# Next layer's norm and first weights made in the last down projection, rotary tables in the load stage, output projections begun by parts

## The reference

```python
    for l in range(DEPTH):
        h = rms_norm(x, norm_mix[l])
        z = h @ w_in[l]
        ...
        mix = jnp.concatenate([o_att, o_hg.astype(x.dtype), o_cv], axis=-1)
        x = x + mix @ w_out[l]

        h = rms_norm(x, norm_mlp[l])
        x = x + jnp.square(jax.nn.relu(h @ w_mlp_in[l])) @ w_mlp_out[l]
    return x
```

## Time and profile before

| | us |
|---|---|
| median of 3 runs | 4067.52 |
| lowest, highest | 4065.33, 4071.44 |
| the profiled execution | 4068.66 |
| its span, first to last instruction | 4066.5 |
| PE busy in it | 3733.8 (92%) |
| DVE, ACT, POOL busy | 2072.0, 1319.8, 1283.6 |

### The profile page before, as it was taken

One profiled execution on the slowest core, in us unless ns is written; L12 is line 12 of the kernel. 1 busy time (PEld: TensorE's weight loads), 2 busy tenths in 40 slices (PEclk: granted clock), 3 DMA queues, 4 the chain that ended last, 5 costly groups with the idle time before them and its releaser, 6 DMA issues. The chain is left out here.

```text
span 4066.5 us, 46227 instructions
## 1 busy us (share of the span) xinstructions
PE 3733.8 (92%) x17918; PEld 2842.7 (70%) x17918; DVE 2072.0 (51%) x2990; ACT 1319.8 (32%) x2225; POOL 1283.6 (32%) x522
## 2 busy tenths in 40 slices
PE   7888999887899979999999989998899999989997
PEld 5555888665578857676777668886657777668885
DVE  4886555398654533533263465443352255345453
ACT  5344111343421121434333421112254433332112
POOL 2202444330144423132323244442113232224442
PEclk9889999997999989999999999999999999899998
DMA  3101333220023232121212123333212122113322
GB/s 111 52 11 42 99 94 93 74 63 16 26 94 94 93 108 86 36 64 57 81 55 73 47 78 94 98 93 112 59 32 78 58 72 68 57 59 95 97 93 67
DMA packets 80145, 292.58 MB, mean 72 GB/s; under 512 B 9616, under 2 KB 10928, under 8 KB 79408
## 3 DMA queue, kind: packets, MB, share of 16 engines
q1 hardware_dynamic: 77136, 278.49, 22.0%
q10 hardware_dynamic: 2784, 11.03, 0.8%
HBM read 285.30 MB, written 2.10 MB: 71 GB/s over the span
## 5 line engine op out<-in xcount | busy, mean ns | idle before, releaser
L207 POOL TENSOR_TENSOR w_lo<-w_raw,w_hi 128x1024 fp32r<-128x1024 f32 x518 | 1283.4, 2478 | 2736.7 <-ACT w_hi L193 2736.6
L193 ACT ACTIVATE w_hi<-w_raw 128x1024 fp32r<-128x1024 f32 x518 | 549.1, 1060 | 1828.7 <-PE acc L244 1757.8
L242 PE MATMUL acc<-hH,w_hi 128*128 128x512 f32 x1840 | 778.5, 423 | 130.9 <-DVE hL L305 70.1
L244 PE MATMUL acc<-hL,w_hi 128*128 128x512 f32 x1840 | 732.0, 398 | 0.0
L243 PE MATMUL acc<-hH,w_lo 128*128 128x512 f32 x1840 | 731.7, 398 | 0.0
L242 PEld LDWEIGHTS acc<-hH,w_hi 128*128 128x128 f32 x1840 | 355.5, 193 | 232.1 <-issue 111.7
L275 DVE TENSOR_TENSOR xT<-acc,xT 128x512 f32<-128x512 f32 x160 | 110.7, 692 | 639.5 <-PE acc L244 639.5
L242 PE MATMUL acc<-H,w_hi 128*128 128x512 f32 x1024 | 405.8, 396 | 5.9 <-issue 4.2
L243 PEld LDWEIGHTS acc<-hH,w_lo 128*128 128x128 f32 x1840 | 355.4, 193 | 76.5 <-issue 12.0
L244 PEld LDWEIGHTS acc<-hL,w_hi 128*128 128x128 f32 x1840 | 353.7, 192 | 78.0
L242 PE MATMUL acc<-midH,w_hi 128*128 128x512 f32 x1024 | 403.7, 394 | 4.2 <-issue 4.2
(11 more groups left out here) (325 smaller groups left out, 4578.5 us busy)
## 6 DMA issues: line engine op xcount, KB each, us to landing
w_raw<-in_stream SPq DMA_DIRECT2D x518, 512.0 KB, 3.5
cw<-in_cmpw ACTq DMA_DIRECT2D x2, 2048.0 KB, 7.9
mixed<-in_cmpw ACTq DMA_DIRECT2D x2, 2048.0 KB, 14.0
x_tok<-in_x SPq DMA_DIRECT2D x1, 2048.0 KB, 9.0
out<-f_tok SPq DMA_DIRECT2D x4, 512.0 KB, 2.6
stack<-Z ACTq DMA_DIRECT2D x8, 128.0 KB, 3.6
stack<-Z ACTq DMA_DIRECT2D x8, 127.8 KB, 3.7
masks_f<-in_masks SPq DMA_DIRECT2D x1, 960.0 KB, 10.8
```

Of the source, the lines that this page charges most:

```text
L193: act.activation(w_hi[:, u % WB, 0:w], w_raw[:, u % 2, 0:w], ACT.Copy).then_inc(hi_split, 1)
L207: pool.tensor_tensor(w_lo[:, u % WB, 0:w], w_raw[:, u % 2, 0:w], w_hi[:, u % WB, 0:w], ALU.subtract)\
L242: pe.matmul(acc[n % 2][:, :], wh, H[:, k, :], start=(k == 0), stop=False)
L244: last = pe.matmul(acc[n % 2][:, :], wh, Lo[:, k, :], start=False, stop=(k == nk - 1))
```

## The change

1. **Norm of the next layer in the last `down`.** `mlp_act` and `mlp_dve` do in the last group `down3` what `out` does: after each `add_to_x` the tile is scaled with the next layer's norm weights (`norm_next`, new columns of `vec`), squared, split into `hH`, `hL`, and the squares are added. A layer begins with one matmul over the added squares (`sum_squares`) and the factor (`rstd_act`), and PE waits for no k part. The buffers `tmp`, `pair`, `yt` are now allocated once.
2. **First weights of the next layer.** `load_next` loads units 0 and 1 of the next layer (new inputs `next1`, `next2`) behind the last units, `split_hi_next` and `split_lo_next` split unit 0. The next layer splits unit 1 first and loads from unit 2 on.
3. **Load stage.** It now also makes the second kind's tables (own buffers `cos2`, `sin2`), the first layer's norm, its unit 0 and the load of unit 1. x comes in two halves, and waits are split by what is needed. `start_second` is gone.
4. **`out` by parts.** Tiles 0 and 1 are each made in two pieces, early k of both, then late k of both (`Group.some`). In a first layer the early k are 4, 5, 0, 1, 2 and the late 3, 6, 7, each with its own wait. In a second layer the early k are 0 to 3; `take_last` splits each tile of `mixed` right after its sum.
5. **`store_result`** has its squares already, releases each `f_y` tile singly, transposes by halves of the width, and stores 8 pieces in place of 4.

```diff
-                        pe.wait_ge(lo_split, u + 1)
+                        if u:
+                            pe.wait_ge(lo_split, u)
...
+            def some(self, tile, ks, ready, begin, end):
+                u, t, n = self.tiles[tile]
...
+                for j, k in enumerate(ks):
+                    ready(k)
...
+        def out_pe(units, early, late, ready):
             out_tiles = Group(units, "out")
+            for ks in (early, late):
+                for tile in range(2):
+                    out_tiles.some(tile, ks, ready, ks is early, ks is late)
+            del out_tiles.tiles[0:2]
             out_tiles.products()
...
+        def load_next(units, source, L):
+            n = len(units)
+            for u in range(2):
+                last_user = n - 2 + (u - n) % 2
+                sp.wait_ge(lo_split, last_user)
+                sp.dma_start(w_raw[:, u, :], source[bass.ds(L, 1), u].rearrange("a p n -> (a p) n"))\
+                    .then_inc(next_loaded[u], 16)
+            for u in range(2):
+                sp.wait_ge(next_loaded[u], 16)
+        def split_hi_next(units):
+            n = max(x[3] for u, x in enumerate(units) if u % WB == 0)
+            act.wait_ge(acc_ready[n % 2], n // 2 + 1)
+            act.wait_ge(next_loaded[0], 16)
+            act.activation(w_hi[:, 0, :], w_raw[:, 0, :], ACT.Copy).then_inc(hi_split, 1)
...
+            def added(k):
+                n = first + k
+                ahead.split_ahead(1)
+                if k == NK - 1:
+                    split_hi_next(units)
+                act.wait_ge(acc_free[n % 2], n // 2 + 1)
+            scale_act(1, gcol, y, sq, added)
...
+        def add_and_scale(r, tiles, y, hi, lo, sq):
+            for k in range(NK):
+                tiles.evacuate(add_to_x, 1)
+                if k:
+                    scale_dve(r, y, hi, lo, k - 1)
+                    add_square(r, sq, k - 1)
+            scale_dve(r, y, hi, lo, NK - 1)
+            add_square(r, sq, NK - 1)
...
                     def _(pe):
                         finish(pe, "start")
                         first_in = Group(units, "first_in")
-                        first_in.products(1, h_ready(0), square_sums(0, pair))
+                        sum_squares(pair)
                         first_in.products()
...
                         finish(pe, "att")
-                        after(pe, stages, "att", act_finished, dve_finished)
-                        out_pe(units, pair)
+                        pe.wait_ge(conv_mean, 2)
+                        pe.wait_ge(conv_rstd, 1)
+                        def out_ready(k):
+                            if k < 4:
+                                pe.wait_ge(att.o_free, k + 1)
+                            if k >= 6:
+                                pe.wait_ge(conv_split, k - 5)
+                        out_pe(units, [4, 5, 0, 1, 2], [3, 6, 7], out_ready)
...
                     def _(act):
-                        split_hi(units, 0)
                         split_hi(units, 1)
+                        act.preload_act_table_set(LOG_EXP)
+                        rstd_act(1)
+                        split_hi(units, 2)
                         act.wait_ge(vec_loaded, 16)
-                        scale_act(0, V1["norm_mix"], yt, pair)
-                        split_hi(units, 2)
...
                         def take_last(i, a, free, value):
                             dve.wait_ge(gate_opened, 3 * NK + i + 1)
                             add_branch(3, i, Z0[:, i, :], a, free, value)
+                            dve.wait_ge(branch_mixed, 3 * NK + i + 1)
+                            link(dve, dve.tensor_copy(hH[:, i, :], mixed[:, i, :]))
+                            dve.tensor_tensor(hL[:, i, :], mixed[:, i, :], hH[:, i, :], ALU.subtract).then_inc(out_split, 1)
                         Group(units, "mix3").evacuate(take_last)
-                        for k in range(NK):
-                            split_dve(hH[:, k, :], hL[:, k, :], mixed[:, k, :])
...
         load_start()
         with nc.Fori(0, DEPTH) as L:
             first_layer(L)
-        start_second()
         with nc.Fori(0, DEPTH) as L:
             second_layer(L)
         store_result()
```

More of the change, by code:

```diff
@@ L349, in h_ready @@
             return lambda k: pe.wait_ge(h_split, NK * r + k + 1)
-        def square_sums(r, sq):
-            def sums(k):
-                pe.wait_ge(sq_ready, NK * r + k + 1)
-                pe.matmul(B[0][:, :], ones, sq[:, k % 2, :], start=(k == 0), stop=(k == NK - 1)).then_inc(sq_summed, 1)
-            return sums
         def split_dve(hi, lo, src):
@@ L390, in mlp_dve @@
                 Group(units, f"up{b}").evacuate(hidden)
-                Group(units, f"down{b}").evacuate(add_to_x)
+                if b < FB - 1:
+                    Group(units, f"down{b}").evacuate(add_to_x)
+            add_and_scale(1, Group(units, f"down{FB - 1}"), y, hH, hL, sq)
         def finish(eng, name):
@@ L866, in _ @@
                             act.wait_ge(v_turned, k + 1)
                             act.activation(xT[:, k, :], B[k % 2][:, :], ACT.Copy).then_inc(v_ready, 1)
+                            act.wait_ge(v_ready, k + 1)
+                        scale_act(0, V1["norm_mix"], yt, pair, turned)
+                    @block.gpsimd
+                    def _(pool):
+                        pool.wait_ge(hi_split, 1)
+                        pool.tensor_tensor(w_lo[:, 0, :], w_raw[:, 0, :], w_hi[:, 0, :], ALU.subtract)
@@ new lines, in _ @@
+                        link(dve, dve.tensor_scalar(n[:, :], n[:, :], -to_whole, None, ALU.add))
+                        for part in parts:
+                            link(dve, dve.scalar_tensor_tensor(ang[:, :], n[:, :], -part, ang[:, :], ALU.mult, ALU.add))
+                        dve.tensor_scalar(ang[:, :], ang[:, :], -edge, edge, ALU.max, ALU.min).then_inc(angle_ready, 1)
+                        for k in range(NK):
+                            scale_dve(0, yt, hH, hL, k)
+                            add_square(0, pair, k)
@@ L1107, in _ @@
                         out_act(units, V1["norm_mlp"], yt, pair)
-                        mlp_act(units)
+                        mlp_act(units, V1["norm_next"], yt, pair)
                     @block.vector
@@ L1578, in _ @@
                         finish(pe, "mix3")
-                        after(pe, stages, "mix3", dve_finished)
-                        out_pe(units, pair)
+                        out_pe(units, [0, 1, 2, 3], [4, 5, 6, 7], lambda k: pe.wait_ge(out_split, k + 1))
                         mlp_pe(units, H2, L2, midH, midL, pair)
@@ L1722, in _ @@
                         finish(act, "mix3")
-                        after(act, stages, "mix3", dve_finished)
                         out_act(units, V2["norm_ff"], yt, pair)
-                        mlp_act(units)
+                        mlp_act(units, V2["norm_next"], yt, pair)
                     @block.vector
```

304 lines of the change are left out of this document (157 added, 147 removed).

## The result

The changed kernel takes **3999.82 us** (median of 4 runs, 3995.95 to 4000.05) against 4067.90 (4 runs, 4065.33 to 4071.44): ratio 0.983, 95% interval 0.9818 to 0.9843. It is 68 us faster where 108 were forecast, and outside the range (3944 to 3978). The profiled execution took 3995.95, 3.9 under the median, with a span of 3994.2; spans are compared with before's 4066.5, 72.3 less.

A forecast was written before the change was run, and what follows sets the result against it. PE, busy for 92% of the span, was taken as the bound, with only its standstills and the low clock after them to win; gains of 107.9 us at edges, load, `out` and store gave 3960 us, range 3944 to 3978.

The forecast's parts named there:

- layer edges: Layer starts: second tile of the next projection earlier by 25.3 us at the change of kind, 11.4 and 13.6 at loop edges.
- start on PE to second tile: From a block's start on PE at a layer start to its second tile: 8.3 us, bounds 7.5 and 9.2.
- behind a jump back: PE idle of about 9.8 us at the two loop edges, 6.5 at the change of kind and the store.
- restart cheap: Rival at layer starts: PE restarts at 1.2 us also behind a jump, about 3950 us; chance 0.05 for below 3946.
- load stage and store: Kernel's two ends: second tile after the load stage 5 us earlier (bounds 2 and 8), the store 9.8 us earlier.
- first layer's `out`: Output projection of first layers, made by parts: PE no longer idles for DVE's last splits, 6.9 us each, 13.8 together.
- low clock at its start: Unknown at the first layers' `out`: PE might start cold although it did not stop, costing up to 2.9 us each.
- `mix3` and `out`: Second layers: splits moved into `mix3`, third tile of `out` 1.3 us late, gain 14.5 us each, 29.0 together.
- everything behind is a steady stream: Whole kernel: an edit's gain is how much earlier the second or third tile of the next projection starts.
- Slower: Rival: PE without rests gets the low clock in dense stretches, the MLPs; 4090 us at 260 us of it; chance 0.02.
- Late weights: Rival after a second layer's start: PE stalls up to 10 us, twice, 3980; 0.11 for this or gains given back.
- Down tiles in down3 over 5.6 us: Sign of a wrong forecast in the last down projection: tiles over 5.6 us mean DVE or ACT too slow.

The follow-up runs named there:

- after_plus224: The changed kernel with 224 unused bytes behind `vec`, so operands stand at 192 modulo 256 as in the kernel before: 3968.35 us.
- before_plus32: The kernel before with 32 unused bytes behind `vec`, every buffer behind it starting 32 bytes later: 4101.51 us, ratio 1.0074.
- after_plus160: The changed kernel with 160 unused bytes behind `vec`, operands behind it at 128 modulo 256 like the weights: 3951.33 us.
- after_w96: The changed kernel with 96 unused bytes ahead of `w_raw` and 64 behind `vec`, moving the weights to 224 modulo 256: 4030.34 us (one run).

## Why the prediction was wrong, point by point

- **Right: layer edges.** Forecast 25.3, 11.4, 13.6, measured 25.8, 11.6, 13.6. The terms behind them held: start on PE to second tile 8.4 to 8.7 at the edges (8.3 forecast), rests of 9.3 and 9.7 behind a jump back (9.8), 5.8 without one (6.5, so this term was 0.7 too dear). The rival "restart cheap" is out.
- **Right: load stage and store.** 6.7 for 5 (its block reached PE at 32.97, not near 34), and 10.1 for 9.8.
- **Right: first layer's `out`.** No low clock at its start: 0.47 us for the first matmul where a cold one takes 0.77. The two places gave 5.4 and 8.3 for 6.9 each. From the end of the last attention product to the MLP alone it is 6.5 each; the rest, -1.0 and +1.8, came in the stretches ahead of `out`, whose instructions are the same.
- **Mis-sized: `mix3` and `out`,** 12.5 in place of 14.5 each, by POOL's blocks of DVE. Inside the bounds (3.3 us late, where 0 to 4.3 were allowed).
- **Wrong: "everything behind is a steady stream".** This is the step that failed. On this sentence the prediction counted only when each stretch starts, and took its length as fixed. Two things contradict it. The pace of the MLP changed by 1.9% because its operands were moved in memory: 26.4 us (and 3.4 more in the tiles on `yH`), against which the text held no term, no bound and no rival. And stretches ahead of `mix3` in the second layers, unchanged in their instructions, took some 5 us longer each at low clock in after_plus224 (the two shown took 5.0 and 1.7 longer in the kernel after). The first alone puts the time out of the range: at the old placement the change measures 3968.35, inside it and 8 over the forecast. At that placement the lines of the table are 10.4 us short of the forecast: 14.5 in the second layers (4 by `mix3` and `out`, 10.5 by the stretches), less 4.1 that the others gave beyond theirs. Of these, 2.6 came in the first layers, where the stretches ahead of `out` happened to be shorter: luck.
- **The rivals.** "Slower" named the dense stretches as the place, but by the clock, and that was granted in full there. Late weights did not happen: no rest of PE above 2 us stands in front of a tile of a second layer's first projection that was not there before. "Down tiles in down3 over 5.6 us" was written as the sign of a slow DVE; they reached 5.6, but so did every other MLP tile, which points away from the norm.

The diff showed the cause: eight more columns in `vec`, 32 bytes, just what before_plus32 adds. It was read for what these columns hold and not for what they push.

## To carry to other kernels

A declaration that moves other buffers is a part of a change and can take back much of its gain (here 31.5 of 99 us): before judging a change, compare the mean start-to-start time of warm matmuls of stages that it does not touch, and give both kernels the same placement. Where PE streams matmuls that each bring their own weights, try to let moving operand and weights start at the same place modulo 256 bytes; here 160 unused bytes gave 48.5 us, and **after_plus160, at 3951.33 us, beats both kernels**. PE's busy share won't show such a loss, a count of instructions in equal windows does.

## What the runs showed of the hardware

The pace of 128x512 matmuls on 4-byte data with a weight load each depends on the distance between the two operands' starts modulo 256 bytes: 226.9 ns a matmul at distance 0, 229.0 at 64, 233.3 at 96, 234.3 at 160. The Trainium skill says of PE's two read ports that loading the next weights takes no bandwidth from the running matmul (TensorE: Matmul & The Clock Gate, Step-by-step: what each phase is for). If so, the pace would not depend on where the weights start. In these runs it does, by up to 3.3%, or 3.7 at distance 240: moving the weights away from `hH` (after_w96) slowed its tiles from 5.47 to 5.62 us. The measurement decides; whether it is the loading of the next weights that meets the running matmul, and where, no run here shows.
